# A two-layer block on one core: bias copies outermost, another bank for one turned head, high-part products first, squares in two halves, gate products moved

## The reference

```python
# first block
mem = rmsnorm(mem) @ w_mem_kv;  u = rmsnorm(x) @ w_in      # memory keys/values; q, k, v, gates of three mixers
s   = q @ k.T / 8 + rel_bias[bucket(i - j)]                # 8 "moba" heads of 64, causal, softmax
x   = x + (gated sum of three branches @ w_br) @ w_out;  x = x + ffn(x)
# second block, layer 1 (mLSTM and pool)
hm  = mlstm(q, k, v, gates) * sigmoid(om)                  # 4 heads of 256
hm  = rms_norm(hm, per head)
ya  = (hm + skip * xc) * silu(zm)
yb  = (pool_means(xp) @ pool_w) * pool_scale * silu(zp)
x   = x + concat(ya, yb) @ w_out
# second block, layer 2 (MLA)
cq, ckv, kpe, z = rms_norm(x) @ w_in
q   = rms_norm(cq) @ w_uq;  k_nope, v = rms_norm(ckv) @ w_ukv
q, k = rms_norm(q), rms_norm(k)                            # per head: squares of the keys are summed
x   = x + attention(rope(q), rope(k), v) * silu(z) @ w_out
```

## Time and profile before

| | |
|---|---|
| median of 3 runs | 783.31 us (782.39 to 783.81) |
| the profiled execution: its time / its span | 784.3 us / 782.5 us |
| granted TensorE clock, mean | 1.00 |
| PE busy | 771.3 us, 99% of the span |
| PE weight loads busy | 683.1 us, 87% |
| DVE / ACT / POOL busy | 568.2 / 439.1 / 151.0 us |
| DMA | 141.77 MB, mean 181 GB/s |

### The profile page before, as it was taken

How to read it: one execution, slowest core, us unless ns; L and a number is a source line. 1 busy time by engine, 2 the same in 40 slices (tenths; PEclk the granted TensorE clock), 3 DMA queues, 4 the chain that set the end, 5 groups by cost and what they waited for, 6 DMA issues and landing times.

```text
span 782.5 us, 12013 instructions
## 1 busy us (share of the span) xinstructions
PE 771.3 (99%) x4640; PEld 683.1 (87%) x4640; DVE 568.2 (73%) x916; ACT 439.1 (56%) x609; POOL 151.0 (19%) x112
## 2 busy tenths in 40 slices
PE   9999999999999999999999999999999989999998
PEld 8787778888888899999998889999799878978886
DVE  5755565894558678878784469899875896898785
ACT  6854675345444566566563363566656344889751
POOL 0002930000000004444543000534105000007000
DMA  9986544344455465455455536437475416554311
GB/s 339 406 308 230 168 155 162 112 159 162 161 170 207 163 206 203 175 175 203 164 199 179 212 113 228 144 113 255 157 248 183 162 55 215 199 179 161 108 55 54
DMA packets 23364, 141.77 MB, mean 181 GB/s; under 512 B 3692, under 2 KB 4600, under 8 KB 7440
## 3 DMA queue, kind: packets, MB, share of 16 engines
q1 hardware_dynamic: 20160, 134.51, 48.5%
q0 software_dynamic: 1376, 3.43, 1.3%
q10 hardware_dynamic: 1776, 3.10, 1.1%
HBM read 139.96 MB, written 2.64 MB: 182 GB/s over the span
## 4 chain that ended last, share of the span: by engine, by line
PE 77%; DVE 9%; DMA 7%; ACT 2%; issue 2%; POOL 1%; SPq 0%; ACTq 0%; DVEq 0%
PE gemm L497 14%; PE gemm L499 14%; PE gemm L498 14%; PE gemm L503 9%; PE gemm L505 9%; PE gemm L504 9%; DMA raw<-in_weights 3%; DMA bias_rows<-bias_row 3%; DVE wlo L1733 2%; DVE xc L2320 1%; ACT whi L1198 1%; PE head L561 1%; POOL wsum_p L2515 1%; PE head L794 1%; DMA bias<-bias_rows 1%
## 5 line engine op out<-in xcount | busy, mean ns | idle before, releaser
L1733 DVE TENSOR_TENSOR wlo<-raw,whi 128x2048 fp32r<-128x2048 f32 x119 | 277.5, 2333 | 92.8 <-ACT whi L1198 92.5
L1198 ACT CAST whi<-raw 128x2048 fp32r<-128x2048 f32 x120 | 228.9, 1908 | 196.5 <-PE gemm L499 107.7
L497 PE MATMUL gemm<-whi,x0hi 128*128 128x512 f32 (+2 forms) x368 | 145.0, 394 | 0.7 <-DVE wlo L1733 0.7
L499 PE MATMUL gemm<-whi,x0lo 128*128 128x512 f32 (+2 forms) x368 | 141.5, 385 | 0.0
L498 PE MATMUL gemm<-wlo,x0hi 128*128 128x512 f32 (+2 forms) x368 | 141.2, 384 | 0.0
L503 PE MATMUL gemm<-x1hi,whi 128*128 128x256 f32 x400 | 113.6, 284 | 0.1
L505 PE MATMUL gemm<-x1hi,wlo 128*128 128x256 f32 x400 | 113.2, 283 | 0.0
L504 PE MATMUL gemm<-x1lo,whi 128*128 128x256 f32 x400 | 113.2, 283 | 0.0
L497 PEld LDWEIGHTS gemm<-whi,x0hi 128*128 128x128 f32 x368 | 69.1, 188 | 15.5 <-issue 2.0
L499 PEld LDWEIGHTS gemm<-whi,x0lo 128*128 128x128 f32 x368 | 69.1, 188 | 13.6
L498 PEld LDWEIGHTS gemm<-wlo,x0hi 128*128 128x128 f32 x368 | 69.2, 188 | 12.2
(11 more groups left out here) (377 smaller groups left out, 1342.2 us busy)
## 6 DMA issues: line engine op xcount, KB each, us to landing
raw<-in_weights SPq DMA_DIRECT2D x122, 1024.0 KB, 4.8
raw<-in_weights SPq DMA_DIRECT2D x4, 512.0 KB, 6.3
bias_rows<-bias_row POOLq DMA_DIRECT2D x1, 1536.0 KB, 20.8
memt<-in_memt SPq DMA_DIRECT2D x4, 256.0 KB, 5.3
tok<-in_mem SPq DMA_DIRECT2D x1, 1024.0 KB, 7.2
xt<-in_xt SPq DMA_DIRECT2D x2, 512.0 KB, 11.0
xres<-in_x ACTq DMA_DIRECT2D x1, 1024.0 KB, 9.1
bias<-bias_rows POOLq DMA_DIRECT2D x8, 128.0 KB, 4.4
```

What stands on the lines that cost most here:

```text
L497: mm(o, xh, wh, start=start, stop=False)
L499: return mm(o, xl, wh, start=False, stop=stop)
L1198: nc.scalar.copy(whi[:, p % RING, :], raw[:, p % RING, :]).then_inc(s_hi, 1)
L1733: V.tensor_tensor(wlo[:, p % RING, :], raw[:, p % RING, :], whi[:, p % RING, :].bitcast(F32), ALU.subtract).then_inc(s_lo, 1)
```

## The change

- The copy to `bias_rows` has the 128 copies as its outermost dimension, the 8 heads inside; it was the other way round.
- Head 2 of the mLSTM is turned into `A[1]`. Heads 1 and 3 wait for a new signal `s_mread`, given when the bank of head 0 or 1 has been read; heads 0 and 2 wait for no reader.
- Pieces of memkv, qkv, z, om and br are entered when `whi` is there. For the first token half the high x high products of all blocks stand first, then the wait for `wlo`, then the other passes. For ukv and uq (`latent_piece`) this holds for both token halves, and the low part of the latents is waited for only ahead of the last pass.
- ACT squares the keys of the first 128 tokens, then empties the first value chunk, then squares the other 128; DVE sums each half on its own.
- The last two gate products of zp stand behind the first two pool chunks on DVE.
- At the start 12 products of `ones` in place of 16, the blocks of a half piece outside the token halves, and a signal of its own for the first block of inputs.

```diff
@@ -364,6 +367,10 @@
...
             return G[2 * (c % 2) + (1 if c in FOUR else t)]
+        def ml_turned(h):
+            return A[1] if h == 2 else A[2]
@@ -510,15 +517,42 @@
...
                 r = p % RING
-                for t in range(T):
+                ts, end = slice(0, P), len(kbs) - 1
+                pe.wait_ge(s_hi, p + 1)
+                for j, kb in enumerate(kbs):
+                    mm(banks[0][:, 0:width], xh[:, kb, ts], whi[:, r, j * width:(j + 1) * width],
+                       start=first and j == 0, stop=False)
+                piece_ready(p)
+                for j, kb in enumerate(kbs):
+                    mm(banks[0][:, 0:width], xh[:, kb, ts], wlo[:, r, j * width:(j + 1) * width], start=False, stop=False)
+                for j, kb in enumerate(kbs):
+                    i = mm(banks[0][:, 0:width], xl[:, kb, ts], whi[:, r, j * width:(j + 1) * width], start=False,
+                           stop=last and j == end)
+                if mid:
+                    mid()
+                for t in range(1, T):
                     ts = slice(t * P, t * P + P)
...
                                    whi[:, r, ws], wlo[:, r, ws],
-                                   first and j == 0, last and j == len(kbs) - 1)
-                    if t == 0 and mid:
-                        mid()
+                                   first and j == 0, last and j == end)
+                return i
+            def latent_piece(p, c, of, kbs, offs, opens):
+                r = p % RING
+                each = [(t, slice(t * P, t * P + P), n, kb, slice(off, off + 512))
+                        for t in range(T) for n, (kb, off) in enumerate(zip(kbs, offs))]
+                for t, ts, n, kb, ws in each:
+                    mm(bank(c, t)[:, :], cqhi[:, kb, ts], whi[:, r, ws], start=n == 0, stop=False)
+                piece_ready(p)
+                for t, ts, n, kb, ws in each:
+                    mm(bank(c, t)[:, :], cqhi[:, kb, ts], wlo[:, r, ws], start=False, stop=False)
+                if opens:
+                    pe.wait_ge(s_tlo, sum(fills(of)[:2]))
+                for t, ts, n, kb, ws in each:
+                    i = mm(bank(c, t)[:, :], cqlo[:, kb, ts], whi[:, r, ws], start=False, stop=n == len(kbs) - 1)
                 return i
@@ -862,11 +896,11 @@
...
                 pe.wait_ge(s_mn, h + 1)
-                if h >= 1:
-                    pe.wait_ge(s_mya, h)
+                if h in (1, 3):
+                    pe.wait_ge(s_mread, (h + 1) // 2)
                 for j in range(2):
                     for t in range(T):
-                        i = nc.tensor.transpose(A[2][:, j * S + t * P:j * S + t * P + P],
+                        i = nc.tensor.transpose(ml_turned(h)[:, j * S + t * P:j * S + t * P + P],
                                                 hm[h % 2][:, t, j * P:j * P + P], ident[:, :])
@@ -1012,7 +1046,7 @@
...
                 pe.wait_ge(s_memset, 1)
-                for _ in range(16):
+                for _ in range(12):
                     mm(A[2][:, 0:P], ones[:, :], ones[:, :], start=True, stop=True)
@@ -1022,10 +1056,15 @@
...
                         pe.wait_ge(s_hi if half else s_hi0, p + 1)
-                        pe.wait_ge(s_inhi, pair + 1)
+                        if (p, half) == (0, 0):
+                            pe.wait_ge(s_in0, 1)
+                        else:
+                            pe.wait_ge(s_inhi, pair + 1)
                         order_ = [(t, 2 * pair + j, slice((2 * half + j) * 512, (2 * half + j) * 512 + 512))
-                                  for t in range(T) for j in range(2)]
+                                  for j in range(2) for t in range(T)]
                         for t, kb, ws in order_:
+                            if (p, kb, t) == (0, 1, 0):
+                                pe.wait_ge(s_inhi, 1)
                             mm(o[t][:, :], x1hi[:, kb, t * P:t * P + P], whi[:, p % RING, ws], start=kb == 0, stop=False)
@@ -1064,13 +1103,16 @@
...
                     if p == p0(name):
-                        pe.wait_ge(s_tlo, sum(fills(of)[:2]))
+                        pe.wait_ge(s_thi, sum(fills(of)[:2]))
                 if p in (p0("up") + 1, p0("down") + 10, p0("aout") + 7):
...
                     pe.wait_ge(s_inlo, 6 + 2 * (p - p0("qkv")))
-                piece_ready(p)
                 name = [n for n, *_ in PHASES if p0(n) <= p][-1]
+                if name in ("memkv", "qkv", "z", "om", "br", "ukv", "uq"):
+                    pe.wait_ge(s_hi, p + 1)
+                else:
+                    piece_ready(p)
                 i_ = p - p0(name)
@@ -1156,22 +1198,12 @@
...
                     chunk_free(pe, c - 2)
-                    for t in range(T):
-                        ts = slice(t * P, t * P + P)
-                        for j in range(3):
-                            ws = slice(j * 512, j * 512 + 512)
-                            i = passes(bank(c, t)[:, :], cqhi[:, 2 + j, ts], cqlo[:, 2 + j, ts],
-                                       whi[:, r, ws], wlo[:, r, ws], j == 0, j == 2)
+                    i = latent_piece(p, c, "cq", [2, 3, 4], [0, 512, 1024], i_ == 0)
                 elif name == "ukv":
...
                         chunk_free(pe, c - 2)
-                        for t in range(T):
-                            ts = slice(t * P, t * P + P)
-                            for j in range(2):
-                                ws = slice(j * D + n * 512, j * D + n * 512 + 512)
-                                i = passes(bank(c, t)[:, :], cqhi[:, j, ts], cqlo[:, j, ts],
-                                           whi[:, r, ws], wlo[:, r, ws], j == 0, j == 1)
+                        i = latent_piece(p, c, "ckv", [0, 1], [n * 512, D + n * 512], i_ == 0 and n == 0)
                         if n == 0:
@@ -1299,6 +1331,8 @@
...
                         last = nc.scalar.activation(hi[:, kb, :], src[:, kb, :], ACT.Copy, scale=pcol(col, kb))
+                        if name == "mem" and kb == 0:
+                            last.then_inc(s_in0, 1)
                     last.then_inc(s_inhi, 1)
@@ -1443,7 +1477,9 @@
...
                     chunk_free(act, c0("ukv") + 1)
-                    i = nc.scalar.activation(flat, kn_c[:, :, :, :].rearrange("p t h d -> p (t h d)"), ACT.Square)
+                    nc.scalar.activation(xn[:, 0, :], kn_c[:, 0, :, :].rearrange("p h d -> p (h d)"),
+                                         ACT.Square).then_inc(s_csk, 1)
+                    return
                 if n == 1:
@@ -1614,6 +1650,9 @@
...
                             act.wait_ge(s_rs, RS["ckv"])
+                        if n == 3:
+                            nc.scalar.activation(xn[:, 1, :], kn_c[:, 1, :, :].rearrange("p h d -> p (h d)"),
+                                                 ACT.Square).then_inc(s_csq, 1)
                         dst = (kn_c, kn_c, v_c, v_c)[n][:, :, 4 * (n % 2):4 * (n % 2) + 4, :]
@@ -1942,6 +1981,8 @@
...
                     for n in late_chunks(name, p, count_):
+                        if name == "zp" and p == p0("pool"):
+                            continue
                         if name == "up":
@@ -2141,9 +2182,10 @@
...
                         blk = 2 * h + j
-                        i = V.scalar_tensor_tensor(xc[:, blk, :], A[2][:, j * S:j * S + S], pcol("head_g", blk),
+                        i = V.scalar_tensor_tensor(xc[:, blk, :], ml_turned(h)[:, j * S:j * S + S], pcol("head_g", blk),
                                                    xc[:, blk, :], ALU.mult, ALU.add)
-                    order(i)
+                    i.then_inc(s_mread, 1)
+                    dve.wait_ge(s_mread, h + 1)
                     V.tensor_tensor(xc[:, 2 * h:2 * h + 2, :], xc[:, 2 * h:2 * h + 2, :],
@@ -2209,8 +2251,10 @@
...
+                dve.wait_ge(s_csk, 1)
+                V.tensor_reduce(kss[:, 1, 0, :], xn[:, 0, :].rearrange("p (h d) -> p h d", d=P), AX, ALU.add)
                 dve.wait_ge(s_csq, 1)
-                V.tensor_reduce(kss[:, 1, :, :], xn[:, :, :].rearrange("p t (h d) -> p t h d", d=P), AX,
+                V.tensor_reduce(kss[:, 1, 1, :], xn[:, 1, :].rearrange("p (h d) -> p h d", d=P), AX,
                                 ALU.add).then_inc(s_csqr, 1)
@@ -2368,6 +2412,9 @@
...
                     elif name == "pool":
+                        if n == 2:
+                            for k in late_chunks("zp", p, 4):
+                                tanh_gate("zp", k)
                         dve.wait_ge(s_zd, n + 1)
@@ -2469,8 +2516,8 @@
...
             pool.wait_ge(s_rbd, 16)
-            pool.dma_start(scratch.rearrange("h (p n) -> h p n", p=P),
-                           rows_out.unsqueeze(1).broadcast_to([MOBA_H, P, TRI])).then_inc(s_rbd, 16)
+            pool.dma_start(scratch.rearrange("h (p n) -> p h n", p=P),
+                           rows_out.unsqueeze(0).broadcast_to([P, MOBA_H, TRI])).then_inc(s_rbd, 16)
             pool.wait_ge(s_rbd, 32)
...
```

3 lines of the change are left out of this document (added).

## The result

The changed kernel takes **778.81 us** (median of 6 runs, 778.40 to 779.55), the kernel before beside it 782.93 us (6 runs, 782.39 to 783.81): a ratio of 0.9947, interval [0.9934, 0.9960], 4.1 us less. Forecast were 777.5 us in a range of 775.8 to 780.3: the sign and the range held, and of the 5.8 us that the sum gave, about 4.1 came. The profiled execution after took 778.65 us with a span of 776.9; the one before 784.3 and 782.5. Between these two executions the difference is 5.6 us, nearly the sum. So the gap between 5.8 and 4.1 lies in what the profiled execution of before stood for. (One profiled execution of the experiments, that of the new copy alone, ran at a mean granted clock of 0.75 and took 948.82 us; it is left out of that run's median, and of its profile only the length of the copy, 8.5 us, is quoted.)

What follows compares the result with a forecast made beforehand. PE bounds the kernel, busy 99% of the span; only its stalls, 7.5 us plus something at the start, can be gained. Terms sum to 5.8 us: 784.3 to 778.5, less 1.0 for the median, 777.5 us; range 775.8 to 780.3.

Steps and rivals of the forecast that it cites:

- start: Kernel start: with fewer warming products, first real product near 6.7 us and third half piece at 12.6; gain 0.29 us.
- bias: First turned moba probabilities: a faster bias copy removes PE's stall at 76.94 us; gain 1.67 us, 0 if no faster.
- gates and order: First xm piece and last two om pieces: moved gate products and high products first together gain 1.02 us.
- turns: mLSTM turns: head 2's stall of 1.28 us goes, head 3 starts at 642.35, not 643.88; together 1.5 us.
- ukv: First ukv product: high latents are there before PE, low ones are asked for later; gain 0.45 us.
- uq: First uq piece: half the keys' squares move behind the first value chunk; gain 0.88 of 1.34 us, 0.46 stays.
- The om pieces: Last two om pieces: the stall for `wlo` moves behind the fourth product and is 0.4 to 0.6 us.
- The list of stalls: PE's idle times by who ended them, from 76.94 to 697.18 us: 7.5 us, just under 1% of the span.
- The first: Rival: the bias copy isn't faster, its 1.67 us stay and the start's 0.29 is lost; 779.5 us, chance 0.10.
- The second: Rival: om, mLSTM and latent gains are halved; 779.4 us, or 779.7 with the start's lost too; chance 0.12.
- The third: Rival: PE starts at half clock, up to twelve products cost 0.2 us more each; 779.9 us, chance 0.04.
- The fourth: Rival: the copy to `bias_rows` gets slower; at twice its time, 41.6 us, the kernel takes 800.3 us; chance 0.03.

Runs made afterwards that it cites:

- the old turns: Changed kernel with all mLSTM heads turned into one bank, each waiting for the product of the head before; 779.99 us, ratio 0.9963.
- the further version: Changed kernel with four more edits, for the stalls at head 3, uq, ym's turn and the last om piece; 776.97 us, beside the changed kernel 777.20 us.
- the old copy: Changed kernel with the bias copy back in its old order, heads outermost; 778.76 us, ratio 0.9946.
- the old start: Changed kernel with 16 warming products, token halves outside and no signal for the first input block; 778.97 us, ratio 0.9947.
- the old gate products: Changed kernel with the last two zp gate products back in their old place, ahead of the pool chunks; 778.81 us, ratio 0.9947.

## Why the prediction was right, and what in it was not

The way of reading held: PE's starts, not its busy share; the stalls as the thing that can be gained; and, for each, what is late next. The forecast, 777.5 us, was 1.3 us too low. The table gives the parts one by one. "Gained" is the time from one landmark to the next in PE's starts, before less after: the third half piece, the first turned probabilities, the turn of head 0, the turn of head 3, the first ukv product, the last product of the kernel. "First" and "second" are the two profiles of the kernel before.

| part | predicted | gained, first | gained, second | undone by itself, median |
|---|---|---|---|---|
| start | 0.29 | 0.0 | 0.10 | 0.2 (within the spread) |
| bias | 1.67 | 1.67 | 0 | 0 |
| gates and order | 1.02 | 1.26 | 0.85 | order 0.9, gates 0 |
| turns | 1.5 | 1.42 | 1.42 | 1.2 |
| ukv | 0.45 | 0.40 | 0.41 | both orders 0.6 |
| uq | 0.88 | 0.89 | 0.94 | |
| sum | 5.8 | 5.6 | 3.7 | |

The times of the six landmarks behind these figures, in us:

| | half piece | probabilities | head 0 | head 3 | ukv | last |
|---|---|---|---|---|---|---|
| before, first | 12.89 | 76.94 | 619.95 | 643.88 | 684.14 | 778.93 |
| before, second | 13.00 | 75.38 | 617.98 | 641.91 | 682.18 | 777.02 |
| after | 12.90 | 75.28 | 617.03 | 639.54 | 679.40 | 773.30 |

The second profile is the better measure, though it was itself 0.4 us shorter than the median of its runs (782.37 against 782.81). The medians differ by 4.1 us, with an interval of about 1 us either way; the 0.4 us between 3.7 and 4.1 is not resolved.

**The step that failed** is the bias: "I take **1.67 us**". Its mechanism was right in the execution it was read from: the stall is there and is gone after, and the copy done twice shows that a late bias does stall PE. As a term for the median it is 0: the copy's order, put in by itself and taken out by itself, changes neither kernel's median. The step at the end that was to carry the sum over ("the median of the runs is 1.0 us lower than the profiled time", so 1.0 off the result too) kept the whole difference as if both kernels had it. But the profiled execution was longer by that stall: it reached the probabilities at 76.94 us where the second profile has 75.38, 1.56 of the 1.9 us by which the two spans differ. A term that the profiled execution has and the median hasn't must be taken out of both. With 0 in its place the sum is 5.8 - 1.7 = 4.1 us, which is what was measured; that it fits so well owes something to luck, since the start and the om pieces were off as well.

**The start** was 0.29 and came to 0.1 us or nothing. PE's first product did come at 6.78 (forecast 6.7), but its third half piece at 12.90, not 12.6. The forecast took the load of the second half piece as it stood in one profile. ACT began that half piece at 8.41 us in it and at 8.58 after, 0.74 us idle for the DMA; and the second product behind a real wait comes 0.11 us late, which the forecast left out here. The other profiles show the load to be the bound: with the new start the third half piece came at 12.60 us where ACT began at 8.25 (the old turns) and at 13.37 where it began at 9.08 (the further version, again), 4.3 us behind it each time. The rise of PE's pitch isn't fixed either. It came at 6.39 us in the profile before, at 5.54 in the second one and at 5.10 after.

**The om pieces**: a stall behind the fourth product was forecast for the last two. The last has it in the profile after (0.46 us, as forecast 0.4 to 0.6). The one before it varies from execution to execution: 0.53 us in the first profile of the kernel before and none in the second; none after, but about 0.25 us in the profiles of the old copy and the old start (554.37 above). That the gate products give nothing by themselves was said in the prediction ("0.85 us by itself would be given back"), and the two experiments show it from both sides.

**The turns** gave 1.42 us between the profiles and 1.2 in the median, for 1.5. Head 3's own stall is 0.90 us, where 0.6 to 0.8 was expected: DVE's norm sets it, as said. **ukv** and **uq** are as forecast, to 0.06 us.

**The list of stalls** that the prediction started from left one out: the turn of ym at 222.19 us, 0.26 us idle behind `x0lo` and so 0.42 us. The change doesn't touch it, so the sum stands; but "7.5 us plus something at the start" was not all there is, and the further version took this one too.

**The rivals.** The first had "the copy isn't faster" and 779.5 us. Its mechanism is wrong, as the copy is faster; but its time was 0.7 us off and the forecast's 1.3, because it left out the same two terms. The second (gains given back) didn't happen: no new stall shows at zm, xm or in the last layer. The third (half clock at the start) didn't show in the profile after: the first four real products start 0.25 us apart, 7.77 - 6.78 for four with the wait in them. But it was nearer than its chance of 0.04 says. In the profiles of the old turns, the old gate products and the further version all 24 warming passes kept the pitch of 0.21 us, and the first real product held up the next by 0.51 to 0.57 us, not 0.31. It was one product or two, 0.2 to 0.3 us in all, and not twelve; PE then waited for the second half piece in the last two of these, and in the first the third half piece came at 12.60 us all the same. (The profile's clock column reads 1.00 from 1.3 us on in all of them, so the half clock at the start is read from the pitch, 0.21 against 0.11 us, and not from a granted clock.) The fourth (a worse copy) is refuted by the copy's length, 12.1 to 16.3 us in nine profiles with one copy in the new order, and 8.5 us in the tenth, the execution of 948.82 us.

The Trainium skill, "DMA: Bandwidth & Descriptors", section "Why a DMA increments its semaphore by 16 and not by 1", let me estimate 10.4 us for a copy on twice the engines. The measured copies agree in direction only: 18.6 to 20.8 us with the heads outermost, and 12.1 to 16.3 with the copies outermost. How many engines took part, no view shows.

## What to carry to other kernels

A stall in a profile belongs to one execution; before it becomes a term, compare the profiled time with the median, and when they differ by about the size of one stall behind a DMA, price that stall at zero or profile again. Two waits on one full engine share one sum: moving its work from the first to the second moves the stall, and only work for the waiting engine that doesn't need the late data takes time off. Where an operand comes in a part that is early and a part that is late, do all that needs the early part first, over as many independent outputs as there are. When a reader waits for a batch of transfers, see whether it needs the whole batch.

## What the runs showed of the hardware

- A long stall cost more than its length. Behind 5.54 us of idle time PE ran at a granted clock of 0.50, with 0.43 us for a product of 512 columns, until about 86.6 us (0.92 as the mean from 86 to 90): 2.6 us on top of 5.7. The Trainium skill, "TensorE: Matmul & The Clock Gate", section "Part 1", calls the throttled state the default, which activity lifts; this trace agrees.
- How long PE stays at its slow pitch after the start differs between executions: with passes back to back from 1.33 us on, the pitch fell from 0.21 to 0.11 us at times between 4.66 and 6.39 us in ten of the thirteen profiles outside the execution of 948.82 us, and in the other three not before the last pass.
- One DMA's length varies from execution to execution far more than the kernel's time does: the same new copy took 12.1, 13.1, 13.4, 13.5, 13.9, 14.7, 15.0, 15.2 and 16.3 us, the old one 18.6, 18.6 and 20.8, while the medians of the kernel before (782.7 to 783.0 on four chips) agree within 0.05%. Slack ahead of the reader keeps this out of the time: with the new order the bias was in time in all nine.
- The first product behind a real wait holds up the next by about 0.1 us more (a row of one product lasts 0.50, not 0.39; a row of four 1.17 to 1.20, not 1.07), so splitting one wait into several isn't quite free. The first product of a piece behind a group of turns has the same 1.17 with no wait in front of it (changed kernel, 63.20 us), so a wait isn't the only thing that does it; the cause is not shown.
